# A hybrid mixer layer on one core: low-rank products in pairs of row groups, and a sixteen-column unit for a and b

## The reference, cut to what matters

```python
p_lru, p_sb, p_gdn, p_rw = _split(h @ w_in[l], MIXER_IN)
# gated DeltaNet: the last 8 columns of its slice, two numbers for each of 4 heads
beta = jax.nn.sigmoid(b_in)
g = -jnp.exp(a_log) * jax.nn.softplus(a_in + dt_bias)
# RWKV-7: low-rank products with 32, 32 and 64 inner columns, each to 256 columns
w_log = -jax.nn.softplus(-(w0 + jnp.tanh(xw) @ w_up)) - 0.5
a = jax.nn.sigmoid(a0 + xa @ a_up)
gate = jax.nn.sigmoid(xg) @ g_up
```

## Time and profile before

| | |
|---|---|
| median of three runs | 1861.43 us |
| profiled execution, its own time | 1861.96 us |
| its span, first to last instruction | 1860.1 us |
| TensorE busy | 1817.7 us (98%) |
| VectorE, GpSimd, ScalarE busy | 1130.8, 830.8, 588.8 us |
| mean granted TensorE clock | 0.997 |

### The profile page before, as it was taken

How to read it: one execution, slowest core, us unless ns; L and a number is a source line. 1 busy time by engine, 2 the same in 40 slices (tenths; PEclk the granted TensorE clock), 3 DMA queues, 4 the chain that set the end, 5 groups by cost and what they waited for, 6 DMA issues and landing times.

```text
span 1860.1 us, 34466 instructions
## 1 busy us (share of the span) xinstructions
PE 1817.7 (98%) x14030; PEld 1456.8 (78%) x14030; DVE 1130.8 (61%) x1706; ACT 588.8 (32%) x957; POOL 830.8 (45%) x954
## 2 busy tenths in 40 slices
PE   6999999999999999999999999999999999999997
PEld 4778777767888888878878788878888888888885
DVE  3855569844555455465544753986666556665656
ACT  4341344353213122222131422543232332233223
POOL 2767556523242233223232747155454455455443
PEclk9999999999999999999999999999999999999999
DMA  9616211224120221230215551011011111111012
GB/s 337 221 48 237 91 56 59 91 91 136 48 92 24 87 95 39 79 102 36 76 55 174 190 215 46 23 46 58 33 68 68 45 45 45 68 45 57 33 68 91
DMA packets 72029, 163.55 MB, mean 88 GB/s; under 512 B 6112, under 2 KB 30816, under 8 KB 71904
## 3 DMA queue, kind: packets, MB, share of 16 engines
q1 hardware_dynamic: 64416, 142.88, 22.2%
q10 hardware_dynamic: 7488, 18.88, 2.7%
HBM read 133.17 MB, written 28.57 MB: 87 GB/s over the span
## 4 chain that ended last, share of the span: by engine, by line
PE 90%; DVE 5%; DMA 1%; issue 1%; ACT 1%; SPq 1%; POOL 1%; ACTq 0%; DVEq 0%; POOLq 0%
PE gbank L778 36%; PE gbank L1335 17%; PE mbank L1436 11%; PE mbank L1119 3%; PE mbank L1335 3%; PE gbank L1259 1%; PE gbank L1319 1%; PE gbank L1349 1%; PE mbank L1349 1%; PE gbank L813 1%; DVE fa L2384 1%; PE gbank L1119 1%; PE mbank L859 1%; PE mbank L1039 1%; PE gbank L880 1%
## 5 line engine op out<-in xcount | busy, mean ns | idle before, releaser
L641 POOL TENSOR_TENSOR w_hi<-w_raw,zero 128x256 fp32r<-128x256 f32 (+1 forms) x260 | 206.3, 823 | 615.1 <-PE gbank L778 594.6
L778 PE MATMUL gbank<-h_hi,w_hi 128*128 128x512 f32 x976 | 392.1, 402 | 0.6 <-POOL w_lo L645 0.6
L778 PE MATMUL gbank<-h_hi,w_lo 128*128 128x512 f32 x976 | 388.9, 398 | 0.0
L778 PE MATMUL gbank<-h_lo,w_hi 128*128 128x512 f32 x976 | 383.8, 393 | 0.0
L691 POOL TENSOR_TENSOR ra<-late,ra 128x256 fp32r<-128x256 f32 x208 | 187.5, 926 | 273.5 <-ACT ra L1924 273.5
L645 POOL TENSOR_TENSOR w_lo<-w_raw,w_hi 128x256 fp32r<-128x256 f32 (+1 forms) x260 | 252.2, 1000 | 5.1
L1436 PE MATMUL mbank<-ffn_a,ra 128*128 128x512 f32 x960 | 221.2, 391 | 3.4 <-POOL ra L691 2.9
L778 PEld LDWEIGHTS gbank<-h_hi,w_hi 128*128 128x128 f32 x976 | 183.4, 188 | 51.9 <-issue 14.2
L778 PEld LDWEIGHTS gbank<-h_hi,w_lo 128*128 128x128 f32 x976 | 183.2, 188 | 40.2 <-issue 0.7
L778 PEld LDWEIGHTS gbank<-h_lo,w_hi 128*128 128x128 f32 x976 | 183.4, 188 | 39.5 <-issue 2.8
L1436 PEld LDWEIGHTS mbank<-ffn_a,ra 128*128 128x128 f32 x960 | 181.2, 189 | 42.0 <-issue 4.2
(11 more groups left out here) (418 smaller groups left out, 2901.8 us busy)
## 6 DMA issues: line engine op xcount, KB each, us to landing
w_raw<-in_w_tail SPq DMA_DIRECT2D x72, 512.0 KB, 3.8
fa<-in_w_ada SPq DMA_DIRECT2D x48, 512.0 KB, 6.6
w_raw<-in_w_in SPq DMA_DIRECT2D x26, 512.0 KB, 4.2
p_scr<-fa ACTq DMA_DIRECT2D x20, 512.0 KB, 2.6
w_raw<-in_w_mix SPq DMA_DIRECT2D x16, 640.0 KB, 4.0
fa<-in_xT SPq DMA_DIRECT2D x16, 512.0 KB, 8.0
w_raw<-in_w_gate SPq DMA_DIRECT2D x16, 512.0 KB, 4.5
sig_scr<-fa ACTq DMA_DIRECT2D x32, 256.0 KB, 2.0
```

What stands on the lines that cost most here:

```text
L641: last = pool.tensor_tensor(hi[:, c], raw[:, c], zero[:, 0:1].to_broadcast([P, w]), ALU.add)
L778: mm = pe.matmul(gb[bank], w, r, start=(q == 0), stop=(q == 3 * ks - 1))
```

## The change

For unit 25, GpSimd splits only 8 columns of each of the 8 tiles, and lays the high part in columns 0 to 7 and the low part in columns 8 to 15 of one sixteen-column weight. TensorE multiplies that with `h_hi` and `h_lo`: 16 matmuls a half (32 in all), with 16 output rows; the low x low term is now included. ScalarE reads 16 rows, TensorE turns 16 rows, and VectorE adds the two groups of 8 columns when it fills `abt` (a copy and an addition).

The low-rank products become eight steps. The first four are pairs: one matmul on partitions 0 to 63 (a tile of w) into `mb[3]` and one on partitions 64 to 127 (a tile of the gate) into `gb[2]`. Step n of these waits until both reads of step n-1 are done. Four single steps follow (the two tiles of a, on partitions 0 to 63), with the banks alternating. Iterations 12, 13 and 14 hold three, three and two steps, and the order of slots and their waits change with it: tile 5 (in step 2) waits for the store of tile 0, which is issued after step 1.

```diff
-        LORA_SLOT = [16, 19, 8, 16, 19, 8]
-        LORA_FREE = [None, ("p_out19", 7), None, ("p_out16", 1), ("p_out19", 8), ("p_out8", 1)]
+        LORA_SLOT = [16, 8, 19, 8, 19, 16]
+        LORA_FREE = [None, None, ("p_out19", 8), ("p_out8", 1), ("p_out19", 7), ("p_out16", 1)]
+        LORA_STEPS = [(0, 0, 4), (0, 1, 4), (1, 0, 5), (1, 1, 5), (2, 0, None), (2, 1, None), (3, 0, None), (3, 1, None)]
+        LORA_ENDS = [2, 4, 6, 8, 9, 10, 11, 12]
...
+            def split_narrow(u):
...
+                pool.wait_ge(sem("gb2_full"), u - 1)
+                pool.tensor_tensor(by_k(w_hi, 0), by_k(w_raw, 0), zero[:, 0:8].rearrange("p (o c) -> p o c", o=1).to_broadcast([P, KT, 8]),
+                                   ALU.add).then_inc(sem("w_hi_set"), 1)
+                pool.wait_ge(sem("w_hi_set"), u + 1)
+                pool.tensor_tensor(by_k(w_hi, 8), by_k(w_raw, 0), by_k(w_hi, 0).bitcast(F32), ALU.subtract).then_inc(sem("w_split"), 1)
...
-                mm = gemm(2 * hf, u % 2, hf, h_hi, h_lo, KT, first, last)
+                if u < 25:
+                    mm = gemm(2 * hf, u % 2, hf, h_hi, h_lo, KT, first, last)
+                else:
+                    for k in range(first // 3, (3 * KT if last is None else last) // 3):
+                        for r in (h_hi, h_lo):
+                            mm = pe.matmul(gb[2 * hf][0:16, :], w_hi[:, u % 2, k * P:k * P + 16], r[:, k, hf * HALF:(hf + 1) * HALF],
+                                           start=(k == 0 and r is h_hi), stop=(k == KT - 1 and r is h_lo))
...
-            def lora_half(n):
-
-                t, hf = divmod(n, 2)
+            def lora_step(n):
+
+                t, hf, other = LORA_STEPS[n]
+                cols = slice(hf * HALF, (hf + 1) * HALF)
...
-                if n >= 2:
-                    pe.wait_ge(sem("lora_read"), n - 1)
-                pe.matmul(gb[2] if hf else mb[3], lora[:, t, :], fa[:, f_slot(L_TILE), hf * HALF:(hf + 1) * HALF], start=True,
+                elif n <= 4:
+                    pe.wait_ge(sem("lora_read"), 2 * n)
+                else:
+                    pe.wait_ge(sem("lora_read"), n + 3 if n > 5 else 8)
+                pe.matmul(lora_bank(n if n >= 4 else 0), lora[0:64, t, :], fa[0:64, f_slot(L_TILE), cols], start=True,
                           stop=True).then_inc(sem("lora_full"), 1)
+                if other is not None:
+                    pe.matmul(gb[2], lora[64:128, other, :], fa[64:128, f_slot(L_TILE), cols], start=True,
+                              stop=True).then_inc(sem("lora_full"), 1)
...
-                        last = pe.transpose(mb[3][:, blk * 8:blk * 8 + 8], fa[0:8, e_slot(25), blk * P:(blk + 1) * P],
-                                            m_("ident")[0:8, 0:8])
+                        last = pe.transpose(mb[3][:, blk * 16:blk * 16 + 16], fa[0:16, e_slot(25), blk * P:(blk + 1) * P],
+                                            m_("ident")[0:16, 0:16])
...
-                t, hf = divmod(n, 2)
-                act.wait_ge(sem("lora_full"), n + 1)
-                if hf == 0 and LORA_FREE[t]:
-                    act.wait_ge(sem(LORA_FREE[t][0]), 16 * LORA_FREE[t][1])
...
+                t, hf, other = LORA_STEPS[n]
+                for k, (t_, bank) in enumerate(((t, gb[2] if n >= 4 and n % 2 else mb[3]), (other, gb[2]))):
+                    if t_ is None:
+                        continue
+                    act.wait_ge(sem("lora_full"), LORA_ENDS[n])
+                    if hf == 0 and LORA_FREE[t_]:
+                        act.wait_ge(sem(LORA_FREE[t_][0]), 16 * LORA_FREE[t_][1])
...
                 if hf == 1:
-                    act.wait_ge(sem("lora_read"), n + 1)
+                    act.wait_ge(sem("lora_read"), LORA_ENDS[n])
                     p_store(LORA_ROW[t], LORA_SLOT[t])
+                    if other is not None:
+                        p_store(LORA_ROW[other], LORA_SLOT[other])
...
-                    dve.tensor_copy(abt[:], mb[3][:, 0:64]).then_inc(sem("ab_read"), 1)
+                    ab_sum = mb[3][:, 0:128].rearrange("p (b w h) -> p b w h", w=2, h=8)
+                    dve.tensor_copy(abt[:].rearrange("p (b h) -> p b h", h=8), ab_sum[:, :, 0]).then_inc(sem("ab_part"), 1)
+                    dve.wait_ge(sem("ab_part"), 1)
+                    dve.tensor_tensor(abt[:].rearrange("p (b h) -> p b h", h=8), abt[:].rearrange("p (b h) -> p b h", h=8), ab_sum[:, :, 1],
+                                      ALU.add).then_inc(sem("ab_read"), 1)
```

More of the change, by code:

```diff
@@ L666, in _ @@
                     split(i * 2 + (4 + s), s, i * 16 + 48)
-            for u in range(10, 26):
+            def split_narrow(u):
+                slot = u % 2
+                by_k = lambda ap, c: ap[:, slot, 0:KT * P].rearrange("p (k c) -> p k c", c=P)[:, :, c:c + 8]
+                pool.wait_ge(sem(f"w_in{slot}"), 16 * (u // 2 + 1))
+                pool.wait_ge(sem("gb2_full"), u - 1)
[3 more added lines that the diff above has]
+                pool.tensor_tensor(by_k(w_hi, 8), by_k(w_raw, 0), by_k(w_hi, 0).bitcast(F32), ALU.subtract).then_inc(sem("w_split"), 1)
+            for u in range(10, 25):
                 split(u, u % 2, 16 * (u // 2 + 1))
+            split_narrow(25)
             for n, kind in enumerate(U_KIND):
@@ L883, in sb_values, with lora_bank @@
                 last.then_inc(sem("sb_o"), 1)
-            def lora_half(n):
-                t, hf = divmod(n, 2)
+            def lora_bank(n):
+                return mb[3] if n % 2 == 0 else gb[2]
+            def lora_step(n):
+                t, hf, other = LORA_STEPS[n]
+                cols = slice(hf * HALF, (hf + 1) * HALF)
                 if n == 0:
@@ L941, in _ @@
                     in_job(j, 0, 12)
-                if 0 <= t < 3:
-                    lora_half(4 * t)
+                if 0 <= t < 3 and 3 * t + 0 < 8:
+                    lora_step(3 * t + 0)
                 if 0 <= t < 4:
@@ L949, in _ @@
                     in_job(j, 12, 24)
-                if 0 <= t < 3:
-                    lora_half(4 * t + 1)
+                if 0 <= t < 3 and 3 * t + 1 < 8:
+                    lora_step(3 * t + 1)
                 if p < PAIRS and SB_STEPS[2 * p][0] >= 4:
@@ L955, in _ @@
                     in_job(j + 1, 0, 12)
-                if 0 <= t < 3:
-                    lora_half(4 * t + 2)
+                if 0 <= t < 3 and 3 * t + 2 < 8:
+                    lora_step(3 * t + 2)
                 if p:
@@ L961, in _ @@
                     in_job(j + 1, 12, 24)
-                if 0 <= t < 3:
-                    lora_half(4 * t + 3)
                 if p:
@@ L1585, in in_read @@
                     act.wait_ge(sem("silu_done"), u - 18)
-                act.activation(fa[:, e_slot(u), hf * HALF:(hf + 1) * HALF], gb[2 * hf], ACT.Copy).then_inc(
+                rows = slice(0, 16) if u == 25 else slice(0, P)
+                act.activation(fa[rows, e_slot(u), hf * HALF:(hf + 1) * HALF], gb[2 * hf][rows], ACT.Copy).then_inc(
                     sem(f"gb{2 * hf}_read"), 1)
@@ L1639, in lora_read @@
             def lora_read(n):
-                t, hf = divmod(n, 2)
-                act.wait_ge(sem("lora_full"), n + 1)
-                if hf == 0 and LORA_FREE[t]:
-                    act.wait_ge(sem(LORA_FREE[t][0]), 16 * LORA_FREE[t][1])
[L1645 to L1649, removed]
+                t, hf, other = LORA_STEPS[n]
[5 more added lines that the diff above has]
+                        act.wait_ge(sem(LORA_FREE[t_][0]), 16 * LORA_FREE[t_][1])
+                    dst = fa[:, LORA_SLOT[t_], hf * HALF:(hf + 1) * HALF]
+                    if t_ < 4:
+                        act.activation(dst, bank, ACT.Sigmoid, bias=pc("rw_w0" if t_ < 2 else "rw_a0", t_ % 2)).then_inc(sem("lora_read"), 1)
+                    else:
+                        act.activation(dst, bank, ACT.Copy).then_inc(sem("lora_read"), 1)
                 if hf == 1:
-                    act.wait_ge(sem("lora_read"), n + 1)
+                    act.wait_ge(sem("lora_read"), LORA_ENDS[n])
                     p_store(LORA_ROW[t], LORA_SLOT[t])
+                    if other is not None:
+                        p_store(LORA_ROW[other], LORA_SLOT[other])
             def gdn_sigmoid(u):
@@ L1683, in _ @@
                     sb_sigmoids(p, 0)
-                if 0 <= t < 3:
-                    lora_read(4 * t)
+                if 0 <= t < 3 and 3 * t + 0 < 8:
+                    lora_read(3 * t + 0)
                 if p:
@@ L1690, in _ @@
                     in_read(j)
-                if 0 <= t < 3:
-                    lora_read(4 * t + 1)
+                if 0 <= t < 3 and 3 * t + 1 < 8:
+                    lora_read(3 * t + 1)
                 if p < PAIRS and SB_STEPS[2 * p][0] >= 4:
                     sb_sigmoids(p, 1)
-                if 0 <= t < 3:
-                    lora_read(4 * t + 2)
+                if 0 <= t < 3 and 3 * t + 2 < 8:
+                    lora_read(3 * t + 2)
                 if p:
```

2 lines of the change are left out of this document (removed).

## The result

The change makes the kernel slower. On one chip, eleven runs each, taken in turn: 1869.70 us median after (1863.76 to 1874.11), 1863.23 before (1860.88 to 1867.71); ratio 1.0034, 95% interval 1.0025 to 1.0043, so 6.5 us. The runs after scatter over 10 us, and their time goes with TensorE's mean granted clock: 1863.76 us at 0.995, 1870 at 0.991, 1874.11 at 0.989. From 0.995 to 0.989 is 0.006 of the span, some 11 us of lost clock, an estimate from these means; the two times lie 10.35 us apart.

What follows compares the result with a forecast made beforehand. TensorE was taken to bound the kernel (90% of the chain), through ScalarE once in each of iterations 12 to 14. -3.65 + 2.69 + 0.27 - 0.41 + 0.05 = -1.05 us took the median 1861.43 to 1860.3; range 1857.5 to 1863.0.

Steps and rivals of the forecast that it cites:

- The a and b unit: Unit 25 on TensorE: 16 fewer matmuls on the path at 0.228 us each, all 3.65 us gained.
- GpSimd's split: Ahead of iteration 11: two small operations in place of eight, costed at nothing and given nothing.
- VectorE's addition: Ahead of the last step's weights: added wait and addition, some 0.4 us, hidden; unhidden it would cost the 0.4.
- the turns: Eight turns on TensorE pass 16 columns and not 8: under 0.1 us more, counted as 0.05.
- Iteration 12: Pair waits for both reads, tile 5's read for a store landing after 2.6 us: values 2.69 us later.
- Iteration 13: Step 3's pair, then singles of steps 4 and 5 back to back: values at 403.63, not 403.36, 0.27 us lost.
- Iteration 14: One low-rank product fewer: values at 409.57, not 409.98, 0.41 us gained.
- The end: Iterations 15, 16 and the stream of 24 gates: +0.05 us, the amount counted for the turns.
- the clock falls: Rival: gaps in iteration 12 drop the granted clock to 0.50, costing 3 us: 1863.3 us; chance 3%.
- the store lands late: Rival, iteration 12: each us of landing beyond 2.6 costs a us; at 6.6 it is 1864.3 us; chance 12%.
- The signs of being wrong: No such gap in iteration 12, landing far from 2.6 us, or low-rank products starting less than 3 us earlier.
- what it wanted to see in the profile: Matmuls at 0.228, low-rank start 3.6 us earlier, overlapping pairs, read at landing, later values, iteration 13 little longer, 14 shorter, clock 1.00.

Runs made afterwards that it cites:

- the unit alone: Kernel before with only the a and b unit changed (32 products of 16 columns), low-rank products as before: 1858.56 us, ratio 0.9981.
- the fourth slot's second run: The change with tile 5 in a slot of its own, so its read doesn't wait for tile 0's store, run again unaltered: 1868.21 us.
- the run with a fourth slot and full rows: The change with tile 5 in its own slot and the single products of steps 4 to 7 on 128 rows: 1862.79 us, run again 1862.29.
- the run with a fourth slot: The change with tile 5 in a slot of its own, so its read doesn't wait for tile 0's store: 1869.77 us, ratio 1.0034.
- the change once more: The change unaltered, run again on the chip of the change with full-row singles: 1867.96 us, ratio 1.0040 to the kernel before.
- the later read: The unit alone, with each iteration's third low-rank product and read behind the second step's turn and copy: 1859.62 us; with gate products moved as well, 1854.43.

## Why the prediction was wrong

It said 1860.3, no change that can be measured; the time is above its range. By its steps:

- **The a and b unit: right.** -3.65 forecast, -3.62 in the change's profile, 3.5 in the runs of the unit alone; 0.229 each for 0.228.
- **GpSimd's split, VectorE's addition, the turns: right.** In the profile after, VectorE adds at 416.79 behind its copy at 416.54, and the values that follow the last turn wait for ScalarE's copies, not for VectorE.
- **Iteration 12: mechanism right, size 0.5 us short.** Step 2's pair waits for both reads (idle 1.30, forecast about one), and tile 5's read is held by the store (releaser `DMA p_scr<-fa`), with the copy and the values behind it. Three terms were low: from the first low-rank product to the turn it is 2.55 us, not 2.35; from there to the read at 391.85 another 0.25 goes to the longer turn and the second pair; the landing took 2.69, not 2.6. By the Trainium skill (DMA: Bandwidth & Descriptors, Anatomy of one DMA) it would have been 3.2, an estimate; 2.69 is nearer to the trace of before.
- **Iteration 13: wrong, 3.25 for 0.27.** The step that failed is the sum's silent term: every product was priced at the clock of before. In the chains, values, scores, pair and six gates take 1.55, 1.16, 1.70 and 2.32 us here, and 0.88, 0.63, 0.86 and 1.59 in the fourth slot's second run, where the clock is still 1.00: 2.8 us are clock, and 0.2 remain.
- **Iteration 14: right** but for 0.2. That is the size of one term: step 7, a single on 64 rows, takes 1.07 us in the chain of the change, and 0.88 on 128 rows in the run with a fourth slot and full rows. Two others cancel: step 6 takes 0.85 for 1.05, the six gates behind it 1.58 for 1.39.
- **The end: wrong, 1.50 for 0.05**, the clock again: the stream of 24 gates takes 6.89 us, 5.68 before and with the unit alone, and the last values 0.69 for 0.44.
- **The rival "the clock falls" is what happened**, given 3% at 1863.3. Its place and the price of the first fall (3 us) were right. Two things were missed. It was priced as one fall, and there are two in the profiled execution, the second worth 1.4 us, and longer ones in executions of its variants (some 24 us). And its condition was judged by the clock of iteration 12 before, 1.00, where TensorE was busy for 7.27 of 7.50 us: a stretch almost without gaps is no evidence for one with gaps. The Trainium skill (TensorE: Matmul & The Clock Gate, Why this matters for your kernels) warns of gaps between bursts of matmuls, of longer ones than these; the traces here agree that idle time lets the clock fall, and differ in the size: 1.30 and 2.17 us in one iteration of the change, 2.5 us alone in the kernel before with one wait put in. The measured gaps decide.
- **The rival "the store lands late": no.** It landed after 2.69, and the run with a fourth slot shows that the wait as such doesn't decide the median.
- **The signs of being wrong:** none of the three that it named came. Of what it wanted to see in the profile, the clock of 1.00 and, with it, the length of iteration 13 failed.

The profiled execution's sum is then -3.6 for the unit, +3.2 for iteration 12, +0.3 for the rest at full clock and +4.2 for the two falls (2.8 and 1.4): 4.1. Its late start (+1.2) and the place of before's profiled execution, 1.3 under its median of 1863.23, nearly cancel; with the 2.55 by which the median run after is longer it is 6.5. That the 2.55 is clock too is argued from the mean clock of the runs (0.991, 0.993), not shown in a trace.

What stays open: why half rows let the clock stay down longer. The medians show that they cost time, with equal gaps and only behind such gaps. The traces say less. In steps of one us from 380 to 500, nine falls stand in kernels whose singles (or all twelve products) have 128 rows, and each lasts 3.4 us; of ten in kernels with half rows, five last 3.4, two 6.8, and the others 17.1, 23.9 and 23.9. The two of 6.8 (the change, and the change once more) begin in iteration 12, ahead of the singles. Nothing in these traces shows by what the chip decides it.

## What to carry to other kernels

A change that makes TensorE wait must be priced twice, for the wait and for the clock that may fall behind it; here the second was the larger. Before a stretch is tightened or stalled, ask what independent products can be put into its gaps: here that, with the later read, brought some 5 us beyond the unit's 3.5, of which the stretch itself shows 3.0. And a wide scatter of the runs with a mean clock that goes along is the sign to look at the clock's column, microsecond by microsecond.

## What was not expected of the hardware

- The granted clock fell to 0.50 behind idle times of 1.30 and 2.17 us in one iteration, and of 2.5 us alone (the wait put into the kernel before). It came back after 3.4 or 6.8 us in these, but only after some 24 us in the fourth slot's second run, where TensorE was busy for all of 405 to 410.
- Whether it falls differs from execution to execution of the same kernel: 1863.76 to 1874.11 us.
- Behind such gaps, products on 64 of 128 rows cost 2.9 and 5.9 us in two pairs of kernels, each on one chip, that differ in nothing else, and 4.1 us by the ratios of a third pair; without such gaps, nothing that could be measured.
